# Attention with two turned tiles a step: the second tile's copy goes between ScalarE's two exponentials

## What is computed

```python
def mla_core(qn, qr, kn, kr, v):
    s = (einsum('bqhd,bkhd->bhqk', qn, kn) + einsum('bqhd,bkd->bhqk', qr, kr)) * MLA_SCALE
    p = softmax(s, axis=-1)
    return einsum('bhqk,bkhd->bqhd', p, v)
...
# window attention: the same with a sink and a band mask
p = softmax_with_sink(concatenate([s_c, s_b], axis=-1), sink_b)
...
# sparse attention: a masked softmax, times a gate per branch
p = exp(s - m) * mask
return p / maximum(sum(p, axis=-1), 1e-20)
```

## Time and profile before

| | us |
|---|---|
| median of 3 runs | 4268.4 |
| lowest and highest | 4262.95, 4271.06 |
| the profiled execution | 4266.7 |
| its span in the trace | 4264.5 |
| TensorE busy in it | 3891.0 |
| VectorE busy | 2230.9 |
| ScalarE busy | 1583.4 |

### The profile page before, as it was taken

How to read it: one execution, slowest core, us unless ns; L and a number is a source line. 1 busy time by engine, 2 the same in 40 slices (tenths; PEclk the granted TensorE clock), 3 DMA queues, 4 the chain that set the end, 5 groups by cost and what they waited for, 6 DMA issues and landing times. The chain is left out here.

```text
span 4264.5 us, 53701 instructions
## 1 busy us (share of the span) xinstructions
PE 3891.0 (91%) x19922; PEld 3027.8 (71%) x19922; DVE 2230.9 (52%) x3880; ACT 1583.4 (37%) x2699; POOL 318.7 (7%) x282
## 2 busy tenths in 40 slices
PE   4998979997999898999899899979889998988998
PEld 3875557776888787865666688856568886657886
DVE  6346567854553574364522556255555525565552
ACT  2235561112442453254611344243434424343431
POOL 0000001111000000100000100104010010401001
PEclk8999989998999999999999999989799999979999
DMA  4100005551222343100022233222023322202322
GB/s 173 57 31 19 1 17 175 195 185 54 96 96 100 107 163 114 65 23 19 1 83 86 79 97 97 95 71 80 11 79 95 102 89 85 75 21 79 98 98 80
DMA packets 86728, 350.82 MB, mean 82 GB/s; under 512 B 9520, under 2 KB 9648, under 8 KB 85680
## 3 DMA queue, kind: packets, MB, share of 16 engines
q1 hardware_dynamic: 72752, 298.53, 21.3%
q0 software_dynamic: 13824, 50.34, 3.5%
HBM read 346.73 MB, written 2.10 MB: 82 GB/s over the span
## 5 line engine op out<-in xcount | busy, mean ns | idle before, releaser
L493 DVE TENSOR_TENSOR split_low<-weight_ring,split_high 128x1024 fp32r<-128x1024 f32 (+1 forms) x456 | 606.2, 1330 | 893.3 <-ACT split_high L485 878.3
L485 ACT ACTIVATE split_high<-weight_ring 128x1024 fp32r<-128x1024 f32 (+1 forms) x474 | 524.7, 1109 | 1037.8 <-PE banks L1342 469.3
L1470 PE MATMUL banks<-normed_high,split_high 128*128 128x512 f32 (+1 forms) x1760 | 653.6, 371 | 77.9 <-DVE normed_low L432 37.9
L1470 PE MATMUL banks<-normed_low,split_high 128*128 128x512 f32 (+1 forms) x1760 | 651.2, 370 | 0.0
L1470 PE MATMUL banks<-normed_high,split_low 128*128 128x512 f32 (+1 forms) x1760 | 650.4, 370 | 0.0
L1470 PEld LDWEIGHTS banks<-normed_high,split_high 128*128 128x128 f32 x1760 | 334.4, 190 | 139.8 <-issue 83.6
L1470 PEld LDWEIGHTS banks<-normed_low,split_high 128*128 128x128 f32 x1760 | 334.5, 190 | 55.6
L1470 PEld LDWEIGHTS banks<-normed_high,split_low 128*128 128x128 f32 x1760 | 334.4, 190 | 55.2
L1342 PE MATMUL banks<-hidden_high,split_high 128*128 128x512 f32 (+1 forms) x880 | 325.1, 369 | 7.2 <-DVE split_low L493 7.2
L1342 PE MATMUL banks<-hidden_high,split_low 128*128 128x512 f32 (+1 forms) x880 | 324.4, 369 | 0.0
L1342 PE MATMUL banks<-hidden_low,split_high 128*128 128x512 f32 (+1 forms) x880 | 324.3, 369 | 0.0
(11 more groups left out here) (301 smaller groups left out, 6641.6 us busy)
## 6 DMA issues: line engine op xcount, KB each, us to landing
weight_ring<-in_up SPq DMA_DIRECT2D x220, 512.0 KB, 3.5
weight_ring<-in_down SPq DMA_DIRECT2D x80, 704.0 KB, 4.0
modulation_ring<-in_ada POOLq DMA_DIRECT2D x80, 512.0 KB, 4.5
weight_ring<-in_merge SPq DMA_DIRECT2D x48, 768.0 KB, 4.5
weight_ring<-in_inputs SPq DMA_DIRECT2D x36, 512.0 KB, 3.5
weight_ring<-in_out SPq DMA_DIRECT2D x32, 512.0 KB, 3.5
latents<-in_ada POOLq DMA_DIRECT2D x16, 512.0 KB, 4.6
weight_ring<-in_xbc SPq DMA_DIRECT2D x16, 512.0 KB, 3.6
```

The lines of the kernel that those rows point to most:

```text
L485: act.activation(k.splits[0][:, (n0 + panel) % RING, 0:width], k.slot(n0 + panel)[:, 0:width], ACT.Copy).then_inc(k.high_ready.sem, 1)
L493: dve.tensor_tensor(k.splits[1][:, s, 0:width], k.ring[:, s, 0:width], k.splits[0][:, s, 0:width].bitcast(F32), ALU.subtract).then_inc(k.l ...
L1470: last = pe.matmul(sums(r, half), w, x, start=(c + j == 0), stop=(c == KT - 1 and j == 2))
```

## The change

On ScalarE, `copy(t - 2, 1)` moves ahead of `exponential(t, 1)`. The condition `per == 2` is as before, so the differential stages keep their order, and so do the waits: the copy waits for its turn (and for the weighing that read its slot last), the exponential for its maximum.

```diff
                 if t < U:
                     exponential(t, 0)
-                    exponential(t, 1)
                 if t >= 2 and per == 2:
                     copy(t - 2, 1)
+                if t < U:
+                    exponential(t, 1)
```

## The result

| | us |
|---|---|
| changed kernel, median of 5 runs | 4243.72 (4240.45 to 4247.24) |
| kernel before, median of 5 runs | 4268.53 (4262.95 to 4271.06) |
| ratio, 95% interval | 0.9944 (0.9930 to 0.9959) |
| profiled execution of the changed kernel | 4247.18, span 4245.0 |

Run once more beside its parts it took 4241.45.

What follows compares the result with a forecast made beforehand. TensorE, busy 91% of the span, bounds the kernel; only its idle waits for ScalarE can go. Window stages 5.8 + 3.5 and sparse 3.4 sum to 12.7 us, latent 0, giving 4256 us; range 4246 to 4265.

Steps and rivals of the forecast that it cites:

- The ring: Window stage, layer 0: turns, copies and exponentials wait on each other; one 0.89 us exponential precedes a copy TensorE needs.
- the bound of 1.62 us: Window stages: the next step's first turn stands at least 1.62 us after the second turn's start.
- periods: Window stages' repeating groups of steps: layer 0's falls from 21.47 to about 19.8 us, layer 1's from 15.72 to about 14.6.
- the window stages: Window attention in both layers of the first model: removed waits for second copies save 5.8 and 3.5 us.
- Latent stages 0: Latent attention: long scores of 768 keys already hide the second copy, so the gain is 0.
- The later exponential costs nothing: ScalarE's second exponential starts a copy later, 0.6 to 0.8 us or more; nobody waits for it, cost taken as 0.
- Table loads 0: ScalarE changes between Exp and Copy twice more per step, but this loads no table: 0 us.
- Sparse stages 3.4 us: Sparse attention: mostly waits for copies of 31-key tiles shrink, 0.43 us each, limited by VectorE's normalising; 1.5 + 1.9 us.
- a rival with 14%: Sparse stages: denser work keeps half of 81 low-clock us at the upper level, 8 us more gain, 4248 us; 14%.
- the forecast's case: Whole kernel: shorter TensorE waits in window and sparse stages save 12.7 us, giving 4256 us; 64%.
- a cold first 30 us: Sparse stage, against the clock rival: its first 30 us stayed at the lower clock with hardly a wait for a copy.
- The second rival (another wait takes the place): Window stages: maxima or normalising end just before the copies, leaving a third of the gain, 4264 us; 17%.

Runs made afterwards that it cites:

- its parts: New order in only the window, sparse or latent stages, old order elsewhere, each against the kernel before: 4256.69, 4255.36 and 4266.44 us.
- latent-only run: New copy order in the two latent stages alone, against the kernel before: 4266.44 us, ratio 0.9998.
- the pair at equal PEclk: Sparse stages at PEclk 0.74: 73.0 us in the old order, 69.6 us in the new order of the changed kernel profiled again.
- the filled kernel before: Kernel before plus 12 unread matmuls of 256 columns ahead of the first score of each sparse stage, against the kernel before: 4279.69 us, ratio 1.0024.
- none blocked: Both copies of a step ahead of both exponentials in all stages with two turned tiles, against the kernel before: 4257.5 us, ratio 0.9974.

## Why the prediction was right in its sign and wrong in its size

- **The ring and the bound of 1.62 us: right.** The exponential in front of the second copy was what TensorE waited for, periods came out at 19.85 and 14.40 against 19.8 and 14.6, the window stages at 9.6 us against 9.3.
- **Latent stages 0: right** (ratio 0.9998). In the latent-only run the stages took 130.6 and 107.1 us, against 130.8 and 107.4. The 6 us longer stage in the first profile is the clock, which the old order meets as well.
- **The later exponential costs nothing: right.** VectorE now waits 2.9 us for exponentials in three waits, two at the end of a latent stage and one at the end of a window stage, and none of it shows in a stage's length: every window stage is as short as foretold or within 0.5 us of it.
- **Table loads 0: right.** The trace of the changed kernel has six of 1283 ns, as before.
- **Sparse stages 3.4 us: the step that failed.** They gave 12.7. Two faults. First and larger, the forecast's sum has no term for the clock. Its reaction was kept apart as a rival with 14%, though its price was about right (8 us for half of the time at the lower level; 6 to 8 measured). It does not replace the forecast's case, it comes on top of it, and the reason given against it (a cold first 30 us) spoke only of the start, not of the dips later in a stage that is warm. Second, the waits were sized too small: 3.4 us, where TensorE's idle time fell by 4.3 and the pair at equal PEclk differs by 6.8 for both stages. A part of this is that the waits were read from a trace of which half ran at 1.2 GHz: where the clock stood higher, in the filled kernel before, waits for copies were 1.0 and 0.3 us longer. The Trainium skill, TensorE: Matmul & The Clock Gate, part 1 and "A second HAM failure mode: psum-queue depth-cycling", says that the gate follows recent activity and that small gaps between groups can make it swing. The runs agree as far as they go: PEclk rose from 0.71 to 0.78 and 0.80 when 16 short copies moved.
- **The range: too narrow above the forecast's gain,** for the same reason: forecast and clock together had no case of their own. 9.6 us of the window stages and 12.8 of the sparse ones are 22.4, which gives 4246; another 2 to 4 us lie outside the six stages or in the scatter (the two profiled executions of the changed kernel differ by 6.4 us), and nothing can be assigned there.

The second rival (another wait takes the place) was not seen in the window stages, where TensorE's waits for VectorE's maxima in layer 0 went only from 4.7 to 5.0 us. In the sparse stages a little of it was: waits for VectorE took back 1.1 of the 5.4 us by which those for copies fell.

## What to carry to other kernels

On an engine that serves two chains, put the operation for which TensorE waits ahead of the one that has slack, and leave just so much of the other work before it as it takes for its input to be ready: one exponential was right, two were too many, none blocked. Where a trace shows a mean granted clock well under 1, count with a gain beyond the gap's length, but not surely: in the sparse stages (0.71 and 0.74) it came, in the window stages (0.93) the gain was the waits and no more. A stage at a lower clock can show shorter waits (5.4 us at a PEclk of 0.71, 6.4 at 0.79, for the same order). Idle time of TensorE that can't be removed can be filled with matmuls that nobody reads: here 8 per stage in four stages gave 13 to 17 us, while 12 in a row ahead of the sparse stages cost 11 (old order) and some 20 us (new order).

## What was not expected of the hardware

- TensorE stayed at 1.2 GHz for 30 us of a sparse stage of the kernel before, though the trace shows it busy for 27.93 of them:

```profile
3015.00:3045.00 30.00, 27.93 (x124) 14.61 (x126) 18.86 (x110) 16.80 (x63) 0.00 (x0) 0.51 0.00 1
```

- The same start of a stage met a low clock of two lengths in two executions of the same kernel: layer 0's latent stage took 130.6 us at 0.99, or 136.9 at 0.93. Two waits of 2.0 us for the maxima stand at its start, and with each of them filled by 2.0 us of matmuls it took 129.1 us at 1.00.
- A short stretch of dense matmuls just before a sparse stage did not pay: it cost 8.1 us and made the rest of the stage 3.0 and 2.2 us shorter in the old order. The clock rose during the filling, and fell again near the stage's start.
